# The last attention's head norms and rotations put between the units of its query projection

## The chip, the cores and the metric

The program runs on one NeuronCore of a Trainium2 chip. The metric is the device time of one execution in microseconds (us). All inputs and outputs are float32, and the whole network below is one launch.

## The reference

Two blocks of two layers each are computed on 512 tokens of width 1024; the second block also carries 256 context tokens. The change touches the last attention only, the mixer of the second block's last layer. Cut to that:

```python
def c_mixer(h_ctx, h_lat, w_in, q_norm_g, k_norm_g, w_out, need_ctx):
    def project(h):
        q, k, v = jnp.split(h @ w_in, [C_WIDTH, C_WIDTH + C_KV_WIDTH], axis=-1)
        q = rms_norm_2(q.reshape(b, t, C_HEADS, C_HEAD_DIM), q_norm_g)      # 8 heads of 128
        k = rms_norm_2(k.reshape(b, t, C_KV_HEADS, C_HEAD_DIM), k_norm_g)   # 2 heads of 128
        return q, k, v.reshape(b, t, C_KV_HEADS, C_HEAD_DIM)
    q_c, k_c, v_c = project(h_ctx)
    q_l, k_l, v_l = project(h_lat)
    q_l, k_l = apply_rope(q_l, cos, sin), apply_rope(k_l, cos, sin)
    k_all = jnp.concatenate([k_c, k_l], axis=1)     # 768 keys
    ... softmax(q k^T / sqrt(128)) v, then @ w_out
```

So each of ten tiles (two of keys over 768 tokens, eight of queries over 512) is divided by the root of its mean square over the 128 features, multiplied by a gain, and, for the 512 latent tokens, turned: `x*cos + rot(x)*sin`.

## The kernel before, in words

The kernel is written engine by engine: each engine (`block.sync`, `block.tensor`, `block.scalar`, `block.gpsimd`, `block.vector`) runs its own list of instructions in the order of the text, and semaphores with explicit counts tie them. Nothing reorders it. Activations lie with the features on the 128 partitions. TensorE is PE, ScalarE is ACT, VectorE is DVE, GpSimd is POOL.

**Split products.** A projection is computed in units of 128 output features. ACT copies a unit's weights (1024 by 128) to a rounded form, `w_hi` (L1250, the helper `f`); DVE subtracts to get the rest, `w_lo` (L1923); PE multiplies hi by hi, hi by lo and lo by hi (L775 to L777), 24 matmuls for 512 tokens. The copies of weights have two places each, taken in turn, so `w_hi` of a unit waits until PE has finished the unit two before it (`act.wait_ge(a_ready...)` in `w_hi`). The result lands in one of two slots of `psA`, from which ACT copies it to SBUF and frees the slot.

**The stage of the change.** After the third MLP (`mlp2`) the hidden state is normed, and PE makes the two key units (`c_k`), the values (`c_v`, 48 float32 matmuls, L726, copied out by DVE at L2503) and the eight query units (`c_q`). Then all engines meet: `meet` drains each engine and waits on `stage_over` until all four have come. Then `head_norms("c_n", 6, 10, ...)` runs on PE, ACT and DVE over the ten tiles, queries first, in pairs: ACT squares a tile (L1250), PE multiplies by a matrix of 1/128 (`mean128`, L726) into `psA`, ACT takes Ln and then Exp of minus a half (the inverse root), DVE multiplies tile, gain and root (L2378), PE multiplies by the rotation matrix (`rot128`, L726) into `psA`, and DVE does three operations (L2388: product with the sine, which reads PSUM; L2389: tile times cosine; L2391: the sum). The mean and rotation products are float32, and the trace has two records for each such matmul. Then there is a second `meet`, and the attention `cat` starts with its first logits. POOL only takes part in the meets here (`BEFORE_MLP3` counts those before it is needed again).

In `block.tensor` the stage reads:

```python
split_linear("c_q", sH[TOK], sL[TOK], LAT)
meet(pe)
head_norms("c_n", 6, 10, lambda m: qC[:, m, :] if m < 8 else kC[:, m - 8, :], sqc, C["mean128"], C["rot128"])
meet(pe)
attention("cat")
```

The whole functions stand here:

Of the kernel before, what the change touches and what calls it, by code (L numbers as in the profile page):

```python
# [7 lines left out]
ALU = mybir.AluOpType  # L8
ACT = mybir.ActivationFunctionType
# [4 lines left out]
KD = D // P  # L14
LAT, CTX = 512, 256
TOK = LAT + CTX
LT, CT = LAT // P, CTX // P
# [13 lines left out]
C_H, C_KV = 8, 2  # L31
# [31 lines left out]
for _name, _n in ROW_SIZES:  # L63
# [18 lines left out]
          ("mlp1", GROUPS * (GH + KD)), ("ln_v3", 1),  # L82
          ("rms0", 1), ("ab", AB_UNITS), ("ab_n", 12), ("lstm", 12),
          ("ab_out", 8), ("mlp2", GROUPS * (GH + KD)),
          ("rms2", 1), ("c_k", 2), ("c_v", 2), ("c_q", 8), ("c_n", 20), ("cat", LT * C_H), ("c_out", 8),
          ("mlp3", GROUPS * (GH + KD))]
PLAN_Q = [("dsa", 4 * DSA_H), ("mla", 4 * MLA_H)]
AHEAD = {"dsa": 2, "mla": 2, "sw": 1}
# [26 lines left out]
def build(nc, d, consts, out):  # L115
    with ExitStack() as ctx:
# [18 lines left out]
        psO = ctx.enter_context(nc.psum_tensor("psO", [P, 1024], F32))  # L135

        C = {name: const[:, a:b] for name, (a, b) in CONST.items()}
        ident = C["ident"]
        eps_ln, eps_rms = C["eps"][:, 0:1], C["eps"][:, 1:2]

        def vec(name, j):
            return vecT[:, ROW[name] + j:ROW[name] + j + 1]

        cursor = [0]

        def area(*shape, at=None):

            if at is not None:
                cursor[0] = at
            n = 1  # L150
            for s in shape:
                n *= s
            v = work[:, cursor[0]:cursor[0] + n]
            cursor[0] += n
            assert cursor[0] <= WORK, cursor[0]
            if len(shape) == 2:
                return v.rearrange("p (a b) -> p a b", b=shape[1])
            if len(shape) == 3:
                return v.rearrange("p (a b c) -> p a b c", b=shape[1], c=shape[2])
            if len(shape) == 4:  # L160
                return v.rearrange("p (a b c e) -> p a b c e", b=shape[1], c=shape[2], e=shape[3])
            return v

        def split(name, shape, at):
# [19 lines left out]
        sH, sL = ({n: split(f"{h}{n}", [P, KD, n], (1 + e) * KD * n) for n in (LAT, TOK)}  # L184
                  for e, h in enumerate(("act_hi", "act_lo")))
# [65 lines left out]

        mixT3 = area(KD, LAT, at=0)
        qC, vC, kC = area(KD, LAT, at=3 * KD * TOK), area(6, 256, at=4 * KD * TOK), area(C_KV, TOK, at=0)
        sqc, rsc, rtc = area(4, TOK), area(2, TOK), area(2, LAT)
        prob3, turn3 = area(2, TOK), area(2, TOK)
        on3 = area(LT, D, at=3 * KD * LAT)


# [10 lines left out]
        stage_over = sem("stage_over")  # L269
        out_set, out_stored = sem("out_set"), sem("out_stored")  # L270
        S = {n: sem(n) for n in (
            "centered", "squared", "sum_ready", "sum_read", "mean_read", "acc_set", "acc_mean", "ple_set", "tile_sum", "norm_set", "acc_zero", "relu_used", "gate_used", "act_hi", "act_split", "w_hi", "w_split", "g_hi", "hidden_set",
            "ada_used", "ada_sum", "row_ready", "row_set", "row_turned", "conv_set", "vec_set", "sqrt_set", "lam_exp", "lam_set",
            "dsa_max", "mla_max", "sw_max", "cat_max", "rope_raw", "root_set", "head_sq",
            "onat_set", "kr_set", "rot_set", "rot_used", "log_set", "row_arg", "carry_arg", "decay_masked", "decay_set", "gain_set", "query_set",
# [53 lines left out]
        def meet(eng):  # L329

            met[eng.engine] = met.get(eng.engine, 0) + 1
            eng.drain().then_inc(stage_over, 1)
            eng.wait_ge(stage_over, 4 * met[eng.engine])
# [25 lines left out]
        w = d["hy_w_in"][0]  # L359
# [20 lines left out]
        w = d["mla_w_down"][0]  # L380
# [3 lines left out]
        w = d["mla_w_uq"][0]  # L384
# [9 lines left out]
        w = d["mla_w_ukv"][0]  # L394
# [6 lines left out]
        w = d["ab_w_in_2"][0]  # L401
# [15 lines left out]
        w = d["c_w_in_2"][0]  # L417
# [118 lines left out]
        def swa_v(qt, kb, h):  # L536
# [19 lines left out]
                        v=lambda qt, kb, h: vC[:, kb, (h // 4) * P:(h // 4) * P + P], prob=prob3,  # L556
                        turn=turn3, onat=lambda qt: on3[:, qt, :], sink=False),
        }
        n_o = {"dsa": 0, "mla": 4, "sw": 12, "cat": 18}
        nmax, rsum, rinv, sink, sarg = small[:, 0:64], small[:, 64:128], small[:, 128:192], small[:, 192:200], small[:, 200:248]  # L560
        sp4, lz, ls, ls2, lacc = (small[:, 232 + 4 * i:236 + 4 * i] for i in range(5))
# [151 lines left out]
        def _(pe):  # L713
# [95 lines left out]
            def split_linear(stage, x_hi, x_lo, n, wait=None, units=KD, behind=None, first=0):  # L809
                if wait:  # L810
                    split_pair(stage, n, x_hi, x_lo, wait)
                for u in range(2 if wait else first, units):
                    pe.wait_ge(S["w_split"], BASE_W[stage] + u + 1)
                    hi, lo = split_place(wH, stage, u), split_place(wL, stage, u)
                    split_products(stage, [u], n, lambda j, k: (hi[:, k, :], lo[:, k, :], x_hi[:, k, :], x_lo[:, k, :]))
                    if behind and u >= 2:
                        behind(u - 2)
                if behind:
                    behind(units - 2)
                    behind(units - 1)  # L820
# [145 lines left out]
            def head_norms(stage, first, n, tile, sq, mean, rot):  # L966

                def norm(m):
                    w = tile(m).shape[-1]
                    pe.wait_ge(S["head_sq"], first + m + 1)  # L970
                    product(stage, norm_product(n, m), [(a, b, [(mean, sq[:, m % 4, a:b])])
                                                        for a, b in ((0, 512), (512, w)) if b > a])

                norm(0)
                norm(1)
                for p in range(0, n, 2):
                    for m in range(p + 2, min(p + 4, n)):
                        norm(m)
                    for m in (p, p + 1):
                        pe.wait_ge(S["rope_raw"], first + m + 1)  # L980
                        product(stage, rope_product(n, m), [(0, LAT, [(rot, tile(m)[:, 0:LAT])])])
# [232 lines left out]
            for step in lstm_steps:  # L1214
                u = step[0]
# [14 lines left out]
            w = weights(pe, "cin", 0)  # L1230
            for g in range(2):
                product("c_v", g, [tokens(w, 256, 512, hraw, t, 256 * (t - 4 * g)) for t in range(4 * g, min(4 * g + 4, 6))])
            split_linear("c_q", sH[TOK], sL[TOK], LAT)
            meet(pe)
            head_norms("c_n", 6, 10, lambda m: qC[:, m, :] if m < 8 else kC[:, m - 8, :], sqc, C["mean128"], C["rot128"])
            meet(pe)
            attention("cat")
            split_linear("c_out", sH[LAT], sL[LAT], LAT, split_here("c_out"), behind=mean_square_of(3, "c_out"))
# [9 lines left out]
        def _(act):  # L1248
# [399 lines left out]
            def head_norms(stage, first, n, tile, sq, rs):  # L1648

                def square(m):  # L1650
                    x = tile(m)
                    f(sq[:, m % 4, 0:x.shape[-1]], x, ACT.Square).then_inc(S["head_sq"], 1)

                square(0)
                square(1)
                for p in range(0, n, 2):
                    for m in range(p + 2, min(p + 4, n)):
                        square(m)
                    if p >= 2:
                        act.wait_ge(S["rope_raw"], first + p)  # L1660
                    roots = [rs[:, m % 2, 0:tile(m).shape[-1]] for m in (p, p + 1)]
                    for m in (p, p + 1):
                        ps, free = get_a(act, stage, norm_product(n, m))
                        f(roots[m % 2], ps[:, 0:roots[m % 2].shape[-1]], ACT.Ln, bias=eps_rms).then_inc(free, 1)
                    act.drain()
                    for m in (p, p + 1):
                        f(roots[m % 2], roots[m % 2], ACT.Exp, scale=-0.5).then_inc(S["root_set"], 1)
# [47 lines left out]

            rms(2, 1, 0, TOK, hraw, sH[TOK], ahead=[("c_k", 0), ("c_k", 1)])
            c_units = [("c_k", m) for m in range(2)] + [("c_q", m) for m in range(8)]
            for n in range(len(c_units) + 2):
                if 2 <= n < len(c_units):
                    w_hi(*c_units[n])  # L1720
                if n >= 2:
                    name, m = c_units[n - 2]
                    ps, free = get_a(act, name, m)
                    dst = kC[:, m, :] if name == "c_k" else qC[:, m, :]
                    f(dst, ps[:, 0:dst.shape[-1]], ACT.Copy).then_inc(free, 1)
            meet(act)
            head_norms("c_n", 6, 10, lambda m: qC[:, m, :] if m < 8 else kC[:, m - 8, :], sqc, rsc)
            meet(act)
            attention("cat", lambda t: mixT3[:, t, :], out="c_out")
            split_linear("c_out", square_of("c_out", LAT), start=2)  # L1730
# [79 lines left out]
        def _(v):  # L1810
# [686 lines left out]


            rms(2, 1, "norm1", 0, TOK, hraw, "cin", ahead=[("c_k", 0), ("c_k", 1)])
            for g in range(2):  # L2500
                n = 4 if g == 0 else 2
                ps, free = get_a(v, "c_v", g)
                nc.vector.tensor_copy(vC[:, 4 * g:4 * g + n, :],  # L2503
                                      ps[:, 0:256 * n].rearrange("p (t c) -> p t c", c=256)).then_inc(free, 1)
            for u in range(8):
                w_lo("c_q", u)
            meet(v)
            head_norms("c_n", 6, 10, lambda m: qC[:, m, :] if m < 8 else kC[:, m - 8, :], rsc, rtc,
                       lambda m: cq8 if m < 8 else vec("ck", 0), C["cosC"], C["sinC"])
            meet(v)  # L2510
            attention("cat")
            gated("c_out", 1, LAT, mixT3)
# [10 lines left out]


LRU_HALF = 8.0 / 2
BEFORE_MLP3 = 2


def host_constants():
# [88 lines left out]
```

## Time and profile before

| | us |
|---|---|
| median of 3 runs | 3305.35 |
| lowest and highest | 3304.45, 3305.71 |
| the profiled execution's own time | 3304.75 |
| its span, first to last instruction | 3303.0 |

| engine | busy, us | share of the span |
|---|---|---|
| PE, matmuls | 3107.6 | 94% |
| PE, weight loads (beside the matmuls) | 2483.6 | 75% |
| DVE | 1632.8 | 49% |
| ACT | 1238.2 | 37% |
| POOL | 155.1 | 5% |

The mean granted TensorE clock is 0.969 of full speed, and the 16 DMA engines move 259.17 MB. The times in the rows below are microseconds from the span's start. A share such as PE's 94% is a mean over very different stages; what a stage is worth is read from its own stretch. The profiled execution's time is 1.75 us above its span, and 0.60 us below the median.

### The profile page before, as it was taken

To read this page: it belongs to the slowest core of one execution; us is meant where nothing else is said; L and a number is where in the kernel's file an instruction comes from. 1 tells how busy PE (TensorE), PEld (TensorE's weight loads), DVE (VectorE), ACT (ScalarE), POOL (GpSimd) and SP (SyncE) were. 2 spreads that over 40 slices of the span, in tenths; PEclk is the share of its full clock that TensorE was granted. 3 is DMA by queue.
4 is the path that set the end of the run, shared out by engine and by line. 5 is a ranking of instruction groups with operands and counts; after the bars stand their busy time and mean duration, and the time that the engine had idled before them with its cause. 6 is when DMAs were issued, how large, how long until landed. Compare 5 with 4: busy or idle time off the path is not lost. (4 is left out here: it accounts for less than half of the span.)

```text
span 3303.0 us, 39562 instructions
## 1 busy us (share of the span) xinstructions
PE 3107.6 (94%) x15192; PEld 2483.6 (75%) x15192; DVE 1632.8 (49%) x2422; ACT 1238.2 (37%) x2046; POOL 155.1 (5%) x142
## 2 busy tenths in 40 slices
PE   6989999999998999998998998999999898899999
PEld 5666677776776677776885777788888775778887
DVE  4763666665454566674415543433333615344344
ACT  2543233335563233336114442423222424543332
POOL 2200000011000000000002001000000100000000
PEclk9969999999999999999998999999999999999999
DMA  5101443433201434431201001112121120022221
GB/s 189 52 25 40 178 157 136 177 106 52 77 1 58 175 124 178 152 109 39 64 26 52 1 1 52 51 51 76 51 76 51 51 77 0 1 77 102 102 87 65
DMA packets 157679, 259.17 MB, mean 78 GB/s; under 512 B 54332, under 2 KB 70074, under 8 KB 157436
## 3 DMA queue, kind: packets, MB, share of 16 engines
q1 hardware_dynamic: 155812, 252.66, 21.8%
q10 hardware_dynamic: 1628, 4.76, 0.4%
q8 instruction: 71, 1.16, 0.1%
q14 instruction: 40, 0.33, 0.0%
q0 software_dynamic: 128, 0.26, 0.0%
HBM read 255.57 MB, written 2.10 MB: 78 GB/s over the span
## 5 line engine op out<-in xcount | busy, mean ns | idle before, releaser
L1250 ACT ACTIVATE w_hi<-wbuf 128x1024 fp32r<-128x1024 f32 (+1 forms) x349 | 368.1, 1057 | 1227.4 <-PE psA L777 1163.9
L775 PE MATMUL psA<-act_hi,w_hi 128*128 128x512 f32 (+1 forms) x1872 | 707.5, 378 | 62.4 <-DVE act_lo L1929 37.1
L1923 DVE TENSOR_TENSOR w_lo<-wbuf,w_hi 128x1024 fp32r<-128x1024 f32 (+1 forms) x349 | 429.3, 1233 | 556.2 <-ACT w_hi L1250 551.0
L776 PE MATMUL psA<-act_lo,w_hi 128*128 128x512 f32 (+1 forms) x1872 | 701.4, 375 | 0.0
L777 PE MATMUL psA<-act_hi,w_lo 128*128 128x512 f32 (+1 forms) x1872 | 700.5, 374 | 0.0
L775 PE MATMUL psA<-hid_hi,w_hi 128*128 128x512 f32 (+1 forms) x1280 | 476.8, 373 | 5.4 <-DVE work L2032 4.5
L776 PE MATMUL psA<-hid_lo,w_hi 128*128 128x512 f32 (+1 forms) x1280 | 472.1, 369 | 0.0
L777 PE MATMUL psA<-hid_hi,w_lo 128*128 128x512 f32 (+1 forms) x1280 | 471.4, 368 | 0.0
L775 PEld LDWEIGHTS psA<-act_hi,w_hi 128*128 128x128 f32 x1872 | 358.8, 192 | 134.7 <-issue 52.1
L777 PEld LDWEIGHTS psA<-act_hi,w_lo 128*128 128x128 f32 x1872 | 357.7, 191 | 62.7
L776 PEld LDWEIGHTS psA<-act_lo,w_hi 128*128 128x128 f32 x1872 | 359.0, 192 | 60.9 <-issue 0.2
L2032 DVE TENSOR_TENSOR work<-work,psA 128x512 f32<-128x512 f32 (+1 forms) x256 | 192.8, 754 | 289.8 <-PE psA L777 282.0
L775 PEld LDWEIGHTS psA<-hid_hi,w_hi 128*128 128x128 f32 x1280 | 241.2, 188 | 65.6 <-issue 18.1
L777 PEld LDWEIGHTS psA<-hid_hi,w_lo 128*128 128x128 f32 x1280 | 241.1, 188 | 41.1
L776 PEld LDWEIGHTS psA<-hid_lo,w_hi 128*128 128x128 f32 x1280 | 241.4, 189 | 38.7
L2054 DVE SCALAR_TENSOR_TENSOR work<-work,small 128x768 f32<-128x768 f32 x224 | 221.7, 1031 | 1.5
L1250 ACT ACTIVATE work<-psA 128x512 f32<-128x512 f32 (+2 forms) x239 | 150.5, 633 | 163.0 <-PE psA L777 146.2
L1250 ACT ACTIVATE work<-psA,small 128x128 f32<-128x128 f32 (+6 forms) x232 | 128.6, 573 | 209.6 <-DVE small L1902 80.3
L2028 DVE TENSOR_TENSOR hid_lo<-work,hid_hi 128x512 fp32r<-128x512 f32 (+1 forms) x128 | 97.1, 759 | 187.0 <-ACT hid_hi L1250 187.0
L740 PE MATMUL psB<-const,work 128*128 128x128 f32 x814 | 143.6, 302 | 41.5 <-ACT work L1250 15.5
L740 PEld LDWEIGHTS psB<-const,work 128*128 128x128 f32 x814 | 102.9, 152 | 95.8 <-issue 36.9
L1250 ACT ACTIVATE work<-work 128x512 f32<-128x512 f32 (+4 forms) x236 | 150.7, 650 | 27.0 <-DVEq L2433 7.4
(271 smaller groups left out, 3562.8 us busy)
## 6 DMA issues: line engine op xcount, KB each, us to landing
wbuf<-in_mlp_w_dram SPq DMA_DIRECT2D x64, 2048.0 KB, 8.2
work<-in_ada_w_dram SPq DMA_DIRECT2D x32, 1536.0 KB, 10.9
wbuf<-in_ab_w_in_dram SPq DMA_DIRECT2D x10, 1024.0 KB, 5.0
wbuf<-in_ple_w_gate_dram SPq DMA_DIRECT2D x4, 2048.0 KB, 7.6
wbuf<-in_hy_w_in_dram SPq DMA_DIRECT2D x3, 2048.0 KB, 13.6
wbuf<-in_c_w_in_dram SPq DMA_DIRECT2D x3, 2048.0 KB, 7.6
wbuf<-in_hy_w_out_dram SPq DMA_DIRECT2D x2, 2048.0 KB, 7.8
wbuf<-in_mla_w_out_dram SPq DMA_DIRECT2D x2, 2048.0 KB, 8.3
```

What stands on the lines that cost most here:

```text
L740: ins = pe.transpose(psB[0:m, s, col:col + k], src, ident[0:k, 0:k])
L775: pe.matmul(psA[:, s, a:b], w_hi, x_hi[:, a:b], start=first, stop=False)
L776: pe.matmul(psA[:, s, a:b], w_hi, x_lo[:, a:b], start=False, stop=False)
L777: ins = pe.matmul(psA[:, s, a:b], w_lo, x_hi[:, a:b], start=False, stop=last)
L1250: return nc.scalar.activation(out, in_, func, **kw)
L1923: tt(split_target(wL, stage, u), unit(v, stage, u, g), split_target(wH, stage, u), ALU.subtract).then_inc(S["w_split"], 1)
L2028: tt(gL[n][:, m, :], hid[n][:, m % 2, :], gH[n][:, m, :], ALU.subtract).then_inc(S["hidden_set"], 1)
L2032: tt(acc[:, j, :], acc[:, j, :], ps[:, 0:n], ALU.add).then_inc(free, 1)
L2054: ins = stt(adas[:, x, :], adaw[:, e, r, :], c, adas[:, x, :], ALU.mult, ALU.add)
```

## The change

It takes the second meeting out and spreads `head_norms` over the query units. The ten tiles have a new order (`C_TILES`): tiles 0 and 1 are the keys, tiles 2 to 9 are query units 0 to 7.

- PE: a mean product is `c_norm(i)`, into `psO[:, 0:512]` (a key's reaches to column 768), and a rotation is `c_rotate(i)`, into `psO[:, 512:1024]`. There is one place for each, no longer two slots of `psA`. `c_norm(i)` waits for the square of tile i and for the root of tile i-1; `c_rotate(i)` waits for tile i to be normalized and, by `c_rot_used`, for DVE to have read the rotation of tile i-1. Ahead of unit 0 stands `c_norm(0)`; behind unit u stand `c_rotate(u-1)` and `c_norm(u+1)`; behind unit 7 the rest follows.
- ACT: behind the copy of a tile comes its square, and then the root (`c_root`) of the tile before it.
- DVE: `w_lo` of query units 0 and 1 moves ahead of the copies of the values. Each later `w_lo(u)` is followed by `c_normalize(u-2)` and, from u = 4 on, `c_turn(u-4)`, the three rotation operations.
- `rtc` and `prob3`/`turn3` move to other places in SBUF, because `act_hi` and `act_lo` are now still in use. `BEFORE_MLP3` is 1. The 20 places of `c_n` in the table of `psA` slots go; the number is even, so later slots stay as they were.

The number of operations of each kind and their shapes are the same in both kernels. The diff, cut:

```diff
-        sqc, rsc, rtc = area(4, TOK), area(2, TOK), area(2, LAT)
-        prob3, turn3 = area(2, TOK), area(2, TOK)
+        sqc, rsc = area(4, TOK), area(2, TOK)
+        rtc = area(2, LAT, at=3 * KD * TOK + KD * LAT)
+        prob3, turn3 = area(2, TOK, at=KD * TOK), area(2, TOK)
...
+        C_TILES = [(8 + m, kC[:, m, :]) for m in range(C_KV)] + [(m, qC[:, m, :]) for m in range(C_H)]
...
-            split_linear("c_q", sH[TOK], sL[TOK], LAT)
-            meet(pe)
-            head_norms("c_n", 6, 10, lambda m: qC[:, m, :] if m < 8 else kC[:, m - 8, :], sqc, C["mean128"], C["rot128"])
+            def c_norm(i):
+                w = C_TILES[i][1].shape[-1]
+                pe.wait_ge(S["head_sq"], 6 + i + 1)
+                if i >= 1:
+                    pe.wait_ge(S["root_set"], 6 + i)
+                for a, b in ((0, 512), (512, w)):
+                    if b > a:
+                        ins = pe.matmul(psO[:, a:b], C["mean128"], sqc[:, i % 4, a:b], start=True, stop=True)
+                ins.then_inc(S["c_mean"], 1)
+            def c_rotate(i):
+                pe.wait_ge(S["rope_raw"], 6 + i + 1)
+                if i < C_KV:
+                    pe.wait_ge(S["root_set"], 6 + C_KV)
+                if i >= 1:
+                    pe.wait_ge(S["c_rot_used"], i)
+                pe.matmul(psO[:, 512:512 + LAT], C["rot128"], C_TILES[i][1][:, 0:LAT], start=True, stop=True).then_inc(S["c_rot"], 1)
+            c_norm(0)
+            for u in range(C_H):
+                split_linear("c_q", sH[TOK], sL[TOK], LAT, None, u + 1, first=u)
+                if u >= 1:
+                    c_rotate(u - 1)
+                c_norm(u + 1)
+            c_rotate(7)
+            c_norm(9)
+            c_rotate(8)
+            c_rotate(9)
...
+            def c_root(i):
+                act.wait_ge(S["c_mean"], i + 1)
+                if i >= 2:
+                    act.wait_ge(S["rope_raw"], 6 + i - 1)
+                root = rsc[:, i % 2, 0:C_TILES[i][1].shape[-1]]
+                f(root, psO[:, 0:root.shape[-1]], ACT.Ln, bias=eps_rms)
+                act.drain()
+                f(root, root, ACT.Exp, scale=-0.5).then_inc(S["root_set"], 1)
...
                     f(dst, ps[:, 0:dst.shape[-1]], ACT.Copy).then_inc(free, 1)
-            meet(act)
-            head_norms("c_n", 6, 10, lambda m: qC[:, m, :] if m < 8 else kC[:, m - 8, :], sqc, rsc)
+                    act.drain()
+                    f(sqc[:, (n - 2) % 4, 0:dst.shape[-1]], dst, ACT.Square).then_inc(S["head_sq"], 1)
+                if n >= 3:
+                    c_root(n - 3)
+            c_root(9)
...
+            w_lo("c_q", 0)
+            w_lo("c_q", 1)
...
-            for u in range(8):
+            def c_normalize(i):
+                m, x = C_TILES[i]
+                v.wait_ge(S["root_set"], 6 + i + 1)
+                stt(x, x, cq8 if m < 8 else vec("ck", 0), rsc[:, i % 2, 0:x.shape[-1]], ALU.mult, ALU.mult).then_inc(S["rope_raw"], 1)
+            def c_turn(i):
+                x = C_TILES[i][1][:, 0:LAT]
+                v.wait_ge(S["c_rot"], i + 1)
+                tt(rtc[:, i % 2, :], psO[:, 512:512 + LAT], C["sinC"], ALU.mult).then_inc(S["c_rot_used"], 1)
+                tt(x, x, C["cosC"], ALU.mult)
+                v.drain()
+                tt(x, x, rtc[:, i % 2, :], ALU.add)
+            for u in range(2, 8):
                 w_lo("c_q", u)
-            meet(v)
-            head_norms("c_n", 6, 10, lambda m: qC[:, m, :] if m < 8 else kC[:, m - 8, :], rsc, rtc,
-                       lambda m: cq8 if m < 8 else vec("ck", 0), C["cosC"], C["sinC"])
+                c_normalize(u - 2)
+                if u >= 4:
+                    c_turn(u - 4)
+            for i in range(6, 10):
+                c_normalize(i)
+                c_turn(i - 2)
+            c_turn(8)
+            c_turn(9)
...
-BEFORE_MLP3 = 2
+BEFORE_MLP3 = 1
```

Where the instructions stand. First DVE before, around the value copies (L2503) and the weight rests of the query units (L1923); L2378 is the normalizing, L2388 the first operation of a turn:

```order
L1929 TENSOR_TENSOR act_lo_52<-work,act_hi_50 128x768 [waits act_hi] x2
L2503 COPY work<-psA 128x1024 [waits a_ready1]
L2503 COPY work<-psA 128x512 [waits a_ready0]
L1923 TENSOR_TENSOR w_lo<-wbuf,w_hi 128x1024 [waits w_landed1,w_hi] x4
L1923 TENSOR_TENSOR w_lo<-wbuf,w_hi 128x1024 [waits w_landed0,w_hi] x4
L2378 SCALAR_TENSOR_TENSOR work<-work,small 128x512 [waits root_set,stage_over]
L2378 SCALAR_TENSOR_TENSOR work<-work,small 128x512 [waits root_set] x3
L2388 TENSOR_TENSOR work<-psA,const 128x512 [waits a_ready1]
```

The same place on DVE in the changed kernel, where L1968 is `w_lo`, L2557 the normalizing and L2563 the first operation of a turn; the last five rows are the round of query unit 4:

```order
L1968 TENSOR_TENSOR w_lo<-wbuf,w_hi 128x1024 [waits w_landed1,w_hi] x2
L2550 COPY work<-psA 128x1024 [waits a_ready1]
L2550 COPY work<-psA 128x512 [waits a_ready0]
L1968 TENSOR_TENSOR w_lo<-wbuf,w_hi 128x1024 [waits w_landed1,w_hi]
L2557 SCALAR_TENSOR_TENSOR work<-work,vecT 128x768 [waits root_set]
L1968 TENSOR_TENSOR w_lo<-wbuf,w_hi 128x1024 [waits w_landed1,w_hi]
L2557 SCALAR_TENSOR_TENSOR work<-work,vecT 128x768 [waits root_set]
L1968 TENSOR_TENSOR w_lo<-wbuf,w_hi 128x1024 [waits w_landed0,w_hi]
L2557 SCALAR_TENSOR_TENSOR work<-work,small 128x512 [waits root_set]
L2563 TENSOR_TENSOR work<-psO,const 128x512 [waits c_rot]
L2564 TENSOR_TENSOR work<-work,const 128x512
L2566 TENSOR_TENSOR work<-work 128x512
```

The eight weight rests stood in one row, and now each is followed by a normalizing and, from unit 4 on, by a turn; the turn of a round stands behind the weight rest of that round.

On PE in the changed kernel, the end of query unit 2 and the start of unit 3 (L778 to L780 are the split products, L1255 the rotation, L1245 the mean):

```order
L778 MATMUL psA<-act_hi_50,w_hi 128x512
L779 MATMUL psA<-act_lo_52,w_hi 128x512
L780 MATMUL psA<-act_hi_50,w_lo 128x512
L1255 MATMUL psO<-work,const 128x512 [waits c_rot_used,root_set,rope_raw]
L1245 MATMUL psO<-work,const 128x512 [waits root_set,head_sq]
L778 MATMUL psA<-act_hi_50,w_hi 128x512 [waits a_free0,w_split]
L779 MATMUL psA<-act_lo_52,w_hi 128x512
```

Before, the rows L775, L776 and L777 of one unit were followed at once by those of the next. Now a rotation with its wait for `c_rot_used` and a mean product stand between them.

## Rows read from the trace of the kernel before

**Rows 1.** The page: the span.

```profile
span 3303.0 us, 39562 instructions
```

**Rows 2.** Busy time and granted clock by stretch, around this stage.

```profile
core 0: us, PE busy (x) PEld busy (x) DVE busy (x) ACT busy (x) POOL busy (x), PEclk, DMA share, GB/s
2629.60:2635.80 6.20, 6.10 (x19) 5.26 (x20) 6.02 (x10) 5.70 (x9) 0.00 (x0) 0.50 0.00 0
...
2672.10:2679.40 7.30, 7.28 (x25) 5.85 (x26) 1.10 (x1) 0.00 (x0) 0.00 (x0) 0.77 0.74 281
2679.40:2717.60 38.20, 38.17 (x169) 31.28 (x167) 7.35 (x6) 9.87 (x13) 0.00 (x0) 1.00 0.31 110
2717.60:2756.80 39.20, 22.07 (x44) 7.20 (x44) 26.52 (x40) 19.54 (x31) 0.00 (x0) 0.94 0.00 0
2756.80:2762.10 5.30, 5.21 (x8) 2.58 (x9) 0.96 (x1) 0.99 (x2) 0.00 (x0) 0.50 0.00 0
```

**Rows 3.** Timeline of PE: start, us, instruction [idle before <-releaser]; projection units.

```profile
2629.70 0.76 PE L775 MATMUL psA<-act_hi,w_hi 128*128 128x512 f32 x1 [6.24 <-DVE act_lo L1929]
...
2669.83 0.38 PE L726 MATMUL psA<-wbuf,work 128*128 128x256 f32 x1
2672.12 0.50 PE L775 MATMUL psA<-act_hi,w_hi 128*128 128x512 f32 x1 [1.91 <-DVE w_lo L1923]
...
2673.87 0.63 PE L775 MATMUL psA<-act_hi,w_hi 128*128 128x512 f32 x1
...
2679.33 0.39 PE L775 MATMUL psA<-act_hi,w_hi 128*128 128x512 f32 x1
...
2717.19 0.39 PE L777 MATMUL psA<-act_hi,w_lo 128*128 128x512 f32 x1
```

**Rows 4.** Timeline of ACT: weight copies and unit copies of the query units.

```profile
2679.59 1.06 ACT L1250 ACTIVATE w_hi<-wbuf 128x1024 fp32r<-128x1024 f32 x1 [28.26 <-PE psA L777]
2680.56 0.58 ACT L1250 ACTIVATE work<-psA 128x512 f32<-128x512 f32 x1
2685.03 1.06 ACT L1250 ACTIVATE w_hi<-wbuf 128x1024 fp32r<-128x1024 f32 x1 [3.89 <-PE psA L777]
```

**Rows 5.** Timeline of DVE: weight rests of the query units.

```profile
2680.69 1.23 DVE L1923 TENSOR_TENSOR w_lo<-wbuf,w_hi 128x1024 fp32r<-128x1024 f32 x1 [7.48 <-ACT w_hi L1250]
```

**Rows 6.** Timeline of PE between the meetings: mean and rotation products, first logits.

```profile
2719.05 1.96 PE L726 MATMUL psA<-work,const 128*128 128x512 f32 x4 [1.48 <-ACT work L1250]
...
2728.16 1.10 PE L726 MATMUL psA<-work,const 128*128 128x512 f32 x2 [1.38 <-DVE work L2388]
...
2741.55 1.53 PE L726 MATMUL psA<-work,const 128*128 128x512 f32 x4 [1.67 <-DVE work L2388]
...
2751.60 1.80 PE L726 MATMUL psA<-work,const 128*128 128x512 f32 x2 [0.87 <-DVE work L2388]
2756.89 1.22 PE L726 MATMUL psA<-work 128*128 128x512 f32 x1 [3.48 <-DVEq L332]
```

**Rows 7.** Timeline of DVE between the meetings.

```profile
2722.54 1.42 DVE L2378 SCALAR_TENSOR_TENSOR work<-work,small 128x512 f32<-128x512 f32 x2 [13.43 <-ACT work L1250]
...
2727.33 0.68 DVE L2388 TENSOR_TENSOR work<-psA,const 128x512 f32<-128x512 f32 x1
2727.94 0.68 DVE L2389 TENSOR_TENSOR work<-work,const 128x512 f32<-128x512 f32 x1
...
2756.07 0.69 DVE L2391 TENSOR_TENSOR work<-work 128x512 f32<-128x512 f32 x1
```

**Rows 8.** Timeline of ACT between the meetings: a logarithm, then exponentials and squares.

```profile
2731.26 0.69 ACT L1250 ACTIVATE work<-psA,const 128x512 f32<-128x512 f32 x1 [1.22 <-PE psA L726]
2732.03 2.62 ACT L1250 ACTIVATE work<-work 128x512 f32<-128x512 f32 x4
```

**Rows 9.** Waits between 2717.6 and 2756.9: who for whom, us, times, longest.

```profile
PE psA L726 <- DVE work L2388: 10.2, 8, 2.4
PE psA L726 <- ACT work L1250: 3.6, 4, 1.6
```

More of the change, by code:

```diff
@@ L84 @@
           ("ab_out", 8), ("mlp2", GROUPS * (GH + KD)),
-          ("rms2", 1), ("c_k", 2), ("c_v", 2), ("c_q", 8), ("c_n", 20), ("cat", LT * C_H), ("c_out", 8),
+          ("rms2", 1), ("c_k", 2), ("c_v", 2), ("c_q", 8), ("cat", LT * C_H), ("c_out", 8),
           ("mlp3", GROUPS * (GH + KD))]
@@ L253, in build @@
         qC, vC, kC = area(KD, LAT, at=3 * KD * TOK), area(6, 256, at=4 * KD * TOK), area(C_KV, TOK, at=0)
-        sqc, rsc, rtc = area(4, TOK), area(2, TOK), area(2, LAT)
-        prob3, turn3 = area(2, TOK), area(2, TOK)
+        sqc, rsc = area(4, TOK), area(2, TOK)
+        assert cursor[0] <= KD * TOK
+        rtc = area(2, LAT, at=3 * KD * TOK + KD * LAT)
+        prob3, turn3 = area(2, TOK, at=KD * TOK), area(2, TOK)
         on3 = area(LT, D, at=3 * KD * LAT)
@@ L271, in build @@
         S = {n: sem(n) for n in (
-            "centered", "squared", "sum_ready", "sum_read", "mean_read", "acc_set", "acc_mean", "ple_set", "tile_sum", "norm_set", "acc_zero", "relu_used", "gate_used", "act_hi", "act_split", "w_hi", "w_split", "g_hi", "hidden_set",
+            "centered", "squared", "sum_ready", "sum_read", "mean_read", "acc_set", "acc_mean", "ple_set", "tile_sum", "c_mean", "c_rot", "c_rot_used", "norm_set", "acc_zero", "relu_used", "gate_used", "act_hi", "act_split", "w_hi", "w_split", "g_hi", "hidden_set",
             "ada_used", "ada_sum", "row_ready", "row_set", "row_turned", "conv_set", "vec_set", "sqrt_set", "lam_exp", "lam_set",
@@ L1723, in _ @@
                     ps, free = get_a(act, name, m)
-                    dst = kC[:, m, :] if name == "c_k" else qC[:, m, :]
+                    dst = C_TILES[n - 2][1]
                     f(dst, ps[:, 0:dst.shape[-1]], ACT.Copy).then_inc(free, 1)
-            meet(act)
-            head_norms("c_n", 6, 10, lambda m: qC[:, m, :] if m < 8 else kC[:, m - 8, :], sqc, rsc)
+                    act.drain()
[3 more added lines that the diff above has]
+            c_root(9)
             meet(act)
```

## The prediction

> **What bounds the kernel now.** PE runs almost without a pause, so I first looked for the places where it does pause. The busy time by stretch [rows 2] shows the query units of this stage as solid PE work: 38.17 of 38.20 us. Behind them lie 39.20 us in which PE is busy 22.07 us, and that figure counts the overlapping ends of matmuls. The timeline of PE [rows 6] says what that stretch is: mean and rotation products with gaps between them, from the first at 2719.05 to the first logits at 2756.89. The list of waits [rows 9] puts 10.2 us of its gaps on DVE (L2388, the operation that frees a rotation's slot) and 3.6 us on ACT. The bound there is the chain PE, ACT, DVE, not any engine. It is the idle time that this change is after, so the question is what the new order makes PE wait for. I counted the stage from the end of the value product (its last record starts at 2669.83 and the next could start at 2670.05) to the first logits: 2756.89 - 2670.05 = 86.8 us [rows 3, 6].
>
> **Prices.** Between two units, 24 split matmuls apart, ACT's weight copies stand 5.44 us apart (2679.59, 2685.03) [rows 4], so a query unit is 5.44 us of PE at full clock. One mean or rotation product over 512 tokens is the difference of four records and two, 1.96 - 1.10 = 0.86 us [rows 6]. A key's mean product has 768 columns; the row with four records that take 1.53 us is one, less the 0.24 us by which the last overlaps what follows: 1.29 us. On DVE a weight rest starts 1.10 us after the weight copy (2679.59 to 2680.69) and takes 1.23 us [rows 4, 5]. A normalizing takes 0.67 us of the queue (1.42 for two, and 0.75 for a single one), and the first operation of a turn 0.68 us [rows 7]. PE starts 0.15 us after that operation has ended (2728.01 to 2728.16) [rows 6, 7]. On ACT a logarithm takes 0.69 us, and the exponential behind it starts 0.08 us later and takes about 0.60 [rows 8].
>
> **The change, part by part.** The number of operations stays, so the sum is a new timetable of this stage.
>
> 1. *The start.* The weight rests of query units 0 and 1 move ahead of the value copies on DVE. Before, PE sat 1.91 us until the first of them was ready, and unit 0 then ran partly at half rate and took 2679.33 - 2672.12 = 7.21 us [rows 3]. Now `c_norm(0)` follows the values at once. The 1.9 us and the 1.8 us both go. POOL and SP have nothing in this stage, and no DMA is issued later than it is needed, as weights for these units have landed.
>
> 2. *PE's own work in line.* Eight units are 43.5 us. Between them stand two key means (2 x 1.29) and, behind units 1 to 6, a rotation and a mean each (6 x 1.72 = 10.3): 56.4 us to the end of unit 7. ACT has some 3.6 us of work per unit and DVE some 4.0, so neither is the bound by its sum.
>
> 3. *The new wait.* The order of instructions shows that behind unit u PE meets `c_rotate(u-1)`, which waits until DVE has read the rotation of tile u-2. DVE does that in the round of `w_lo(u+2)`, behind that weight rest and behind a normalizing. And `w_lo(u+2)` needs `w_hi(u+2)`, which ACT can only write when PE has finished unit u, since the two places of the weights are taken in turn [rows 4]. So for u = 2, 3, 4, 5 PE must sit from the end of unit u through: 0.26 to the weight copy (2679.33 to 2679.59), 1.10, a rest 1.14 (its 1.23 less the overlap with the next), a normalizing 0.67, the turn's first operation 0.68, 0.15 to PE. That is 4.00 us, four times: 16.0 us. Queued behind it on PE are a mean product and the whole next unit. Behind unit 1 there is no such wait (rotation 0 has no predecessor). Behind units 6 and 7 the turns belong to rounds without a weight rest: they wait for a root that is ready 3.3 us after the unit before, well inside the unit's 5.44 us. Unit 7 thus ends at 56.4 + 16.0 = 72.4 us instead of 47.4 (2717.42).
>
> 4. *The tail.* After unit 7: rotation 6 and mean 8 (to 1.72), then ACT's root 8 (result 0.2 later, 0.69 + 0.08 + 0.60: to 3.3), normalizing 8 and the first operation of turn 6 (to 4.8). Only then rotation 7 and mean 9 (4.9 to 6.6), root 9 (to 8.25), normalizing 9 and turn 7's first operation (to 9.65), rotation 8 (to 10.7), turn 8's first operation (10.95 to 11.6), rotation 9 (11.8 to 12.85), three operations and the drain (to 15.1). The logits start 15.15 us behind unit 7 instead of 39.4. The meeting itself cost 0.13 us before (DVE ends at 2756.76), so a meeting less is worth that only.
>
>    Without the clock: 72.4 + 15.2 = 87.6 against 86.8, **0.8 us slower**. The 24 us won in the tail are paid for by work moved in line (12.9), four waits (16.0), less the repaired start (3.9).
>
> 5. *The clock.* No row shows four waits of 4 us in turn. After 1.91 us of idle PE, the granted clock of the next stretch was 0.77 on average: a spell at 1.2 GHz, in which a matmul record takes 0.63 us and not 0.39, and the unit lost 1.8 us [rows 2, 3]. After 6.24 us of idle, 6.2 us were granted 0.50 throughout [rows 2, 3], a loss of 3.1 us. Between these, and nearer the first, I take 2.4 us for each wait: 9.6 us (bounds 7.2 and 12.4, and nothing for a wait that happens to draw no spell: the stretch between the meetings, with gaps of 0.9 to 1.7 us [rows 6], was still granted 0.94 on average [rows 2]). In the tail PE waits three times some 3 us, and four products of 0.86 us stand on the chain; at half rate each costs 0.86 more, 0 to 3.4; I take 1.7. The logits start at half rate before [rows 2] and will do so now.
>
>    The Trainium skill (TensorE: Matmul & The Clock Gate, "HAM oscillation — how this bites in real kernels") says that a loop whose rounds each hold a long wait pays for the return to full clock in every round, and measured 1.67 us at half rate each. By its figure the four waits would cost 4 x 0.83 = 3.3 us and the sum would be 6 us, an estimate. The unit that lost 1.8 us after less than 2 us of idle [rows 3] speaks for the larger price, and the sum goes by the rows.
>
>    **Sum: 0.8 + 9.6 + 1.7 = 12.1 us** on the profiled execution's 3304.75 (span 3303.0 [rows 1]), that is 3316.9, and I give 3317.0. The median of the runs is 0.6 us above that execution, within the runs' own spread of 1.3 us.
>
> **The rivals.**
>
> - *The same waits, a kind clock.* If some waits fall so that no spell at 1.2 GHz follows, the clock costs 0 to 5 us and the kernel ends at 3305.5 to 3310.5; I put it at 3309. For it: the 0.94 just named. Against: these waits are more than twice as long.
> - *The waits are not there, and it is faster.* The mechanism is that of the name: what is three tiles behind is ready in time. The place is `c_rotate(u-1)`. Its price is the 16.0 us and the clock with them: 56.4 + 15.2 = 71.6 against 86.8, 15.2 us faster, 3289.6. It decides at the point where DVE reads the old rotation before unit u ends. For it: DVE has 4.0 us of work in a round of 7.2. Against: DVE works in order, and the turn stands behind a weight rest that cannot start before that unit ends. That is read from the order and from ACT's waits of 3.89 us for PE [rows 4].
> - *It feeds on itself.* If slow products also lengthen the tail and the rounds of units 6 and 7 (a root that is not ready in time), two more waits of 2 to 4 us come, with their spells: 3323 to 3330.
>
> That the change might not do what it says is ruled out by the rows of the order: the products do stand between the units.
>
> **How the numbers follow.** My forecast has 0.68, the kind clock 0.14, the faster case 0.07, the self-feeding one 0.11. The measurement of this kernel can tell about 0.2%, or 6.6 us, from no change: the bounds are 3298.7 and 3312.0. Faster is the second rival, 0.07. Within lie nearly all of the kind clock and a little of the forecast's low end, 0.14. Slower is the rest, 0.79. The range runs from 3307, which takes in most of the kind clock, to 3322, which is the forecast with each clock price at its upper bound (0.8 + 12.4 + 3.4 = 16.6, so 3321.4); outside are the faster case, a part of the self-feeding one and the best of the kind clock. The likeliest case alone spans 3312 to 3321.
>
> **What would show it.** In the new timeline of PE: no idle time between the values and unit 0, and no spell at 1.2 GHz in it; behind units 2 to 5, four times, some 4.0 us of idle released by the turn's first operation (L2563), and a granted clock below 1 behind each; nothing behind units 1, 6 and 7 before rotation 7; the first logits 15 to 18 us behind unit 7. The list of waits should show PE waiting for L2563 some 22 to 25 us in this stage. I am wrong if the gaps are under 2 us, if there are six and not four, or if the clock stays at 1.00.

## The result, and the profile after

The changed kernel takes 3320.02 us (median of 5 runs, 3317.84 to 3322.15); the kernel before takes 3305.71 us in the same comparison (3304.45 to 3310.17). The ratio is 1.0042, with a 95% interval of 1.0027 to 1.0056. The change costs 14.3 us; the forecast was 12.1.

The profiled execution has a span of 3318.2 us against 3303.0 [rows 1], 15.2 us more. The stage, counted from the end of the value product to the first logits, is read from the timeline of PE. These are its mean products (L1245), rotations (L1255) and first logits (L729); the split matmuls of the units lie between the rows:

```profile
2671.55 1.45 PE L1245 MATMUL psO<-work,const 128*128 128x512 f32 x4
2678.32 1.46 PE L1245 MATMUL psO<-work,const 128*128 128x512 f32 x4
2685.07 1.02 PE L1255 MATMUL psO<-work,const 128*128 128x512 f32 x2
2685.93 1.02 PE L1245 MATMUL psO<-work,const 128*128 128x512 f32 x2
...
2696.22 2.05 PE L1255 MATMUL psO<-work,const 128*128 128x512 f32 x2 [3.82 <-DVE work L2563]
2698.05 1.92 PE L1245 MATMUL psO<-work,const 128*128 128x512 f32 x2
...
2710.33 2.04 PE L1255 MATMUL psO<-work,const 128*128 128x512 f32 x2 [3.82 <-DVE work L2563]
...
2724.24 2.05 PE L1255 MATMUL psO<-work,const 128*128 128x512 f32 x2 [3.82 <-DVE work L2563]
...
2738.06 2.05 PE L1255 MATMUL psO<-work,const 128*128 128x512 f32 x2 [3.82 <-DVE work L2563]
...
2747.77 1.02 PE L1255 MATMUL psO<-work,const 128*128 128x512 f32 x2
...
2754.95 1.02 PE L1255 MATMUL psO<-work,const 128*128 128x512 f32 x2
2755.81 1.02 PE L1245 MATMUL psO<-work,const 128*128 128x512 f32 x2
2759.78 1.66 PE L1255 MATMUL psO<-work,const 128*128 128x512 f32 x2 [2.95 <-DVE work L2563]
...
2772.35 5.26 PE L729 MATMUL psA<-work 128*128 128x512 f32 x8 [2.18 <-DVEq L334]
```

The stage lasts 2772.35 - 2671.55 = 100.8 us, where it lasted 86.8 [rows 3, 6]: 14.0 of the 15.2 us are here, and the value product already ended 1.5 us later than before, in work that the change does not touch. Four rotations start behind 3.82 us of idle PE, each released by DVE's L2563. Before the first four rows there is no idle time. Unit 7 ends at 2754.95, which is 83.4 us into the stage (47.4 before), and the logits start 17.4 us behind it (39.5 before).

What DVE does in one such wait, from its timeline (unit 2 ended at 2692.23; ACT's weight copy started at 2692.49):

```profile
2693.58 1.23 DVE L1968 TENSOR_TENSOR w_lo<-wbuf,w_hi 128x1024 fp32r<-128x1024 f32 x1 [5.01 <-ACT w_hi L1281]
2694.72 0.75 DVE L2557 SCALAR_TENSOR_TENSOR work<-work,small 128x512 f32<-128x512 f32 x1
2695.38 0.68 DVE L2563 TENSOR_TENSOR work<-psO,const 128x512 f32<-128x512 f32 x1
```

DVE sat idle for 5.01 us, although the rotation that it would read had long been made; the first thing in its queue was the weight rest. The read that frees PE stands third. From the end of the unit to PE's start at 2696.22 it is 3.99 us.

The clock, by stretches of the changed kernel (columns as in [rows 2]): the start up to the first wait, the four rounds behind the waits, unit 7, the tail, the first logits:

```profile
2671.50:2692.20 20.70, 20.70 (x85) 15.63 (x84) 5.00 (x5) 8.95 (x12) 0.00 (x0) 1.00 0.43 156
...
2696.20:2706.40 10.20, 10.18 (x28) 6.66 (x28) 1.16 (x2) 1.32 (x2) 0.00 (x0) 0.71 0.00 0
...
2710.30:2720.20 9.90, 9.87 (x28) 6.52 (x28) 1.17 (x2) 1.32 (x2) 0.00 (x0) 0.72 0.00 0
...
2724.20:2734.10 9.90, 9.86 (x28) 6.41 (x28) 1.19 (x2) 1.32 (x2) 0.00 (x0) 0.73 0.01 2
...
2738.00:2747.80 9.80, 9.74 (x29) 6.59 (x30) 3.85 (x6) 1.32 (x2) 0.00 (x0) 0.74 0.58 212
2747.80:2754.90 7.10, 7.10 (x29) 5.24 (x28) 2.65 (x4) 2.54 (x4) 0.00 (x0) 1.00 0.00 0
2754.90:2772.30 17.40, 8.49 (x13) 2.34 (x12) 9.22 (x14) 3.86 (x6) 0.00 (x0) 0.75 0.00 0
2772.30:2777.60 5.30, 5.25 (x9) 2.64 (x10) 0.96 (x1) 0.99 (x2) 0.00 (x0) 0.53 0.00 0
```

The rounds behind the waits are granted 0.71 to 0.74, and PE is busy in them without a break. A rotation and a mean behind a wait take 2.05 and 1.92 us, not 1.02 each. A rotation, a mean and a unit take 7.17 us at full rate (2685.07 to 2692.24), and the four rounds last 10.1, 9.9, 9.8 and 9.7 us, so the spells at 1.2 GHz cost 10.9 us in all, 2.5 to 3.0 us each. The list of waits of PE in the stage:

```profile
PE psO L1255 <- DVE work L2563: 22.1, 7, 3.8
PE psA L729 <- DVEq L334: 2.2, 1, 2.2
```

Before, PE waited 10.2 us for L2388 and 3.6 for ACT between the meetings [rows 9]. The change took those waits out and put 22.1 us on the same kind of operation.

### The profile page after: what moved, and what is told of

Its sections match the earlier page's. It is cut to its first block, busy times and chain, and to the rows that moved or that the text cites. A ratio compares the mean times of both kernels' runs of the same rounds, so it can differ in the third digit from the quotient of the medians.

```text
span 3318.2 us, 39574 instructions
## 1 busy us (share of the span) xinstructions
PE 3119.2 (94%) x15192; PEld 2490.5 (75%) x15192; DVE 1633.9 (49%) x2422; ACT 1239.2 (37%) x2046; POOL 154.2 (5%) x142
## 4 chain that ended last, share of the span: by engine, by line
PE 86%; DVE 6%; ACT 4%; issue 1%; DVEq 1%; DMA 1%; ACTq 1%; POOLq 0%; PEldq 0%; PEld 0%; SPq 0%
PE psA L778 23%; PE psA L779 22%; PE psA L780 22%; PE psB L743 3%; PE psA L729 3%; PE psA L904 2%; PE psO L921 2%; ACT work L1281 2%; PE psO L1045 1%; PE psO L866 1%; PE psA L965 1%; ACT w_hi L1281 1%; DVE w_lo L1968 1%; PE psA L794 1%; DVE work L2077 1%
## 5 line engine op out<-in xcount | busy, mean ns | idle before, releaser
L778 PE MATMUL psA<-act_hi,w_hi 128*128 128x512 f32 (+1 forms) x1872 | 712.8, 381 | 60.3 <-DVE act_lo L1974 37.0
L1968 DVE TENSOR_TENSOR w_lo<-wbuf,w_hi 128x1024 fp32r<-128x1024 f32 (+1 forms) x349 | 430.4, 1236 | 580.5 <-ACT w_hi L1281 575.1
L780 PE MATMUL psA<-act_hi,w_lo 128*128 128x512 f32 (+1 forms) x1872 | 700.9, 374 | 0.0
L778 PE MATMUL psA<-hid_hi,w_hi 128*128 128x512 f32 (+1 forms) x1280 | 476.8, 373 | 5.4 <-DVE work L2077 4.5
L780 PE MATMUL psA<-hid_hi,w_lo 128*128 128x512 f32 (+1 forms) x1280 | 471.5, 368 | 0.0
L778 PEld LDWEIGHTS psA<-act_hi,w_hi 128*128 128x128 f32 x1872 | 359.5, 192 | 134.8 <-issue 54.4
L780 PEld LDWEIGHTS psA<-act_hi,w_lo 128*128 128x128 f32 x1872 | 358.5, 192 | 63.2
L778 PEld LDWEIGHTS psA<-hid_hi,w_hi 128*128 128x128 f32 x1280 | 241.2, 188 | 65.7 <-issue 18.2
L780 PEld LDWEIGHTS psA<-hid_hi,w_lo 128*128 128x128 f32 x1280 | 241.1, 188 | 41.3
## 6 DMA issues: line engine op xcount, KB each, us to landing
work<-in_ada_w_dram SPq DMA_DIRECT2D x32, 1536.0 KB, 10.9
```

What stands on the lines that cost most here:

```text
L778: pe.matmul(psA[:, s, a:b], w_hi, x_hi[:, a:b], start=first, stop=False)
L780: ins = pe.matmul(psA[:, s, a:b], w_lo, x_hi[:, a:b], start=False, stop=last)
L1968: tt(split_target(wL, stage, u), unit(v, stage, u, g), split_target(wH, stage, u), ALU.subtract).then_inc(S["w_split"], 1)
```

## The experiments

Eight kernels ran, in two groups of four, each beside the kernel before, whose median was 3305.84 us in the first group and 3306.03 in the second. The stage is measured as above in each one's profile.

| kernel | median, us | against before, 95% | stage, us | unit 7's end, us | logits behind it, us |
|---|---|---|---|---|---|
| before | 3305.71 | 1 | 86.8 | 47.4 | 39.5 |
| the change | 3320.02 | 1.0042 (1.0027 to 1.0056) | 100.8 | 83.4 | 17.4 |
| turn before the weight rest | 3293.56 | 0.9961 (0.9945 to 0.9976) | 74.9 | 56.6 | 18.4 |
| turn first everywhere | 3286.97 | 0.9946 (0.9930 to 0.9961) | 67.3 | 56.6 | 10.8 |
| two places for a rotation | 3290.05 | 0.9952 (0.9937 to 0.9968) | 69.3 | 56.6 | 12.7 |
| filled waits | 3310.17 | 1.0013 (1.0004 to 1.0022) | 88.8 | 72.8 | 16.0 |
| the start alone | 3302.23 | 0.9991 (0.9982 to 1.0000) | 84.2 | 43.8 | 40.4 |
| two tiles behind | 3283.76 | 0.9930 (0.9917 to 0.9944) | 66.9 | 57.4 | 9.4 |
| two behind, filled end | 3287.19 | 0.9937 (0.9924 to 0.9951) | 66.8 | 57.4 | 9.4 |
| half-filled waits | 3312.28 | 1.0018 (1.0009 to 1.0028) | 94.0 | 76.1 | 17.9 |

(In the row of the start alone, the stage is counted from the first query matmul at 2675.82, since PE goes from the values straight to it.)

### The turn before the weight rest

```diff
             for u in range(2, 8):
+                if u >= 4:
+                    c_turn(u - 4)
                 w_lo("c_q", u)
                 c_normalize(u - 2)
-                if u >= 4:
-                    c_turn(u - 4)
```

> The changed kernel, but in each round DVE makes the turn first and the weight rest behind it, so the old rotation is read before the unit ends. My theory (PE waits four times for a turn that is queued behind a weight rest that needs the unit's end): the four gaps of 3.8 us go, and with them the spells at 1.2 GHz behind them (10.9 us); the stage from the value product's end to the first logits falls from 100.8 us to 56.4 + 17.4 = 73.8, and the time from 3320 to 3291 to 3294, under the kernel before. The rival (PE is slowed by float32 products standing between the units, whatever DVE does) expects the gaps to shrink little and at most 5 us off: 3315 or more.

It took 3293.56 us, in the expected range. The same three DVE operations, in another place of the same round, and all four gaps are gone. Two stretches of its profile, the units and the tail:

```profile
2672.50:2729.10 56.60, 56.60 (x226) 42.15 (x225) 25.41 (x33) 25.02 (x36) 0.00 (x0) 1.00 0.32 112
2729.10:2747.40 18.30, 9.38 (x13) 2.53 (x11) 9.25 (x14) 3.86 (x6) 0.00 (x0) 0.72 0.00 0
```

PE is busy in all of the 56.60 us, at full clock. The forecast's timetable had 56.4 for this work without waits. So float32 products between the units cost their own 0.86 and 1.29 us and 0.2 us beyond that in all, and the rival that blamed them falls. Against the change, the stage is 25.9 us shorter: 16.0 of waits and 10.9 of spells, less 1.0 by which this tail is longer.

### The turn first everywhere

```diff
             for i in range(6, 10):
-                c_normalize(i)
                 c_turn(i - 2)
+                c_normalize(i)
```

This stands on top of the edit before.

> As the first, and the turn stands ahead of the normalizing in the last rounds too, so that rotation 7 and mean 9 do not wait for root 8 and normalizing 8. My theory: rotation 7 starts about 2 us behind unit 7 and no longer 4.8, and the logits start 11 to 13 us behind unit 7 and not 17.4: 3286 to 3289. If the tail is bound by the sum of DVE's own operations, not by their order, it stays within 1 us of the first.

It took 3286.97 us. The tail fell from 18.4 to 10.8 us, just under the expected 11 to 13. The last products in its timeline of PE:

```profile
2728.43 1.02 PE L1255 MATMUL psO<-work,const 128*128 128x512 f32 x2
2729.29 1.02 PE L1245 MATMUL psO<-work,const 128*128 128x512 f32 x2
2730.33 1.10 PE L1255 MATMUL psO<-work,const 128*128 128x512 f32 x2
2731.88 1.10 PE L1245 MATMUL psO<-work,const 128*128 128x512 f32 x2 [0.45 <-ACT work L1281]
2733.27 1.10 PE L1255 MATMUL psO<-work,const 128*128 128x512 f32 x2 [0.29 <-DVE work L2563]
2735.93 1.10 PE L1255 MATMUL psO<-work,const 128*128 128x512 f32 x2 [1.56 <-DVE work L2563]
2739.21 4.54 PE L729 MATMUL psA<-work 128*128 128x512 f32 x8 [2.18 <-DVEq L334]
```

Rotation 7 starts 1.9 us behind unit 7's end, where it started 4.8 in the change. The long way through mean 8, root 8, normalizing 8 and the turn, twice over, was a matter of order as well. Part of the 7.6 us is the clock: the last four products take 1.10 us each here, and 1.78 to 2.05 us each in the run before.

### Two places for a rotation

```diff
-                if i >= 1:
-                    pe.wait_ge(S["c_rot_used"], i)
-                pe.matmul(psO[:, 512:512 + LAT], C["rot128"], C_TILES[i][1][:, 0:LAT], start=True, stop=True).then_inc(S["c_rot"], 1)
+                if i >= 2:
+                    pe.wait_ge(S["c_rot_used"], i - 1)
+                pe.matmul(psB[:, i % 2, :], C["rot128"], C_TILES[i][1][:, 0:LAT], start=True, stop=True).then_inc(S["c_rot"], 1)
...
-                tt(rtc[:, i % 2, :], psO[:, 512:512 + LAT], C["sinC"], ALU.mult).then_inc(S["c_rot_used"], 1)
+                tt(rtc[:, i % 2, :], psB[:, i % 2, :], C["sinC"], ALU.mult).then_inc(S["c_rot_used"], 1)
```

DVE's order is that of the change.

> The changed kernel with DVE's order left as it is, but with two places for a rotation (in psB, by the tile's parity), so that a rotation waits for the turn two tiles back. It tells the single place apart from the order on DVE. My theory: the gaps go just as in the first, 56.4 us to the end of unit 7, and the tail is about 13 us: 3286 to 3291. If the order on DVE is itself the bound, the gaps stay: 3315 or more.

It took 3290.05 us, and unit 7 ends 56.6 us into the stage. The rotations behind units 2 and 3, in its timeline of PE, have no idle time before them:

```profile
2690.24 1.02 PE L1255 MATMUL psB<-work,const 128*128 128x512 f32 x2
...
2697.42 1.02 PE L1255 MATMUL psB<-work,const 128*128 128x512 f32 x2
```

The wait needs both: one place, and a reader that is queued behind something that needs the end of the unit. Either remedy takes it out whole.

### The waits filled

```diff
+                if 2 <= u <= 5:
+                    keep_clock(psB[:, 0, :], 4)
                 if u >= 1:
                     c_rotate(u - 1)
                 c_norm(u + 1)
```

> The changed kernel with four idle-filling float32 matmuls (their result is not used) ahead of the rotation behind units 2 to 5: 3.44 us of PE work in each wait of 3.8. The waits stay, the clock should not fall. My theory: the rotations start within 0.3 us of where they do now, counted from their unit's end, but the rounds last 11.2 us and not 13.8 to 14.1, and the time falls by the clock's 10.9 us to 3308 to 3311. If the clock costs only the 3.3 us by the Trainium skill's figure, 3316 to 3318; if the rounds are long for another reason, no change.

It took 3310.17 us, 9.9 under the change. Two of the four waits in its timeline of PE, with the filling matmuls at L734:

```profile
2697.08 3.60 PE L734 MATMUL psB<-const 128*128 128x512 f32 x8
2701.06 1.10 PE L1255 MATMUL psO<-work,const 128*128 128x512 f32 x2 [0.39 <-DVE work L2565]
2702.00 1.02 PE L1245 MATMUL psO<-work,const 128*128 128x512 f32 x2
2708.31 3.60 PE L734 MATMUL psB<-const 128*128 128x512 f32 x8
2712.30 1.10 PE L1255 MATMUL psO<-work,const 128*128 128x512 f32 x2 [0.38 <-DVE work L2565]
```

The rotation still starts 3.98 us behind the unit's end (2697.08 to 2701.06), so the wait is all there. But the round from one rotation to the next is 11.24 us and not 14.11, and the granted clock from 2697 to 2755 is 1.00. Unit 7 ends 72.8 us into the stage; the forecast had 72.4 without the clock. This measures the two parts apart: unit 7 ends 16.2 us later than where nothing waits (56.6), which is the waiting, and 10.6 us earlier than in the change (83.4), which is what the half rate behind the waits cost. The Trainium skill's figure (TensorE: Matmul & The Clock Gate, "HAM oscillation — how this bites in real kernels"), carried over to these four waits, gave 3.3 us by an estimate; these runs disagree with that and the measurement decides. That every round pays anew, as the page says, agrees: each of the four rounds of the change lost 2.5 to 3.0 us.

### The start alone

```diff
+            w_lo("c_q", 0)
+            w_lo("c_q", 1)
             for g in range(2):
...
-            for u in range(8):
+            for u in range(2, 8):
                 w_lo("c_q", u)
```

This is the kernel before with that one edit.

> The kernel before with one part of the change alone: the weight rests of query units 0 and 1 ahead of the value copies on DVE. My theory: the 1.9 us of idle PE behind the values go, and so does the spell at 1.2 GHz in unit 0 (1.8 us); the stage falls from 86.8 to 83.0 us, the time by 3 to 4 us to 3302. The rival (the gap goes but a spell falls in unit 0 anyway, or the units' start only moves a wait to the second meeting): the stage is 85 or more and the time unchanged within 1 us.

It took 3302.23 us, 3.8 less than the kernel before (3306.03 in that group), though the interval reaches to 1.0000, so the two medians alone hardly show a gain. The trace does. Its first query matmul, first mean product and first logits, in its timeline of PE:

```profile
2675.82 0.58 PE L775 MATMUL psA<-act_hi,w_hi 128*128 128x512 f32 x1
...
2721.21 1.95 PE L726 MATMUL psA<-work,const 128*128 128x512 f32 x4 [1.48 <-ACT work L1250]
...
2759.99 4.26 PE L726 MATMUL psA<-work 128*128 128x512 f32 x8 [3.53 <-DVEq L332]
```

The gap of 1.91 us and the spell in unit 0 went: from the first query matmul to the first mean product it is 45.4 us, where it was 46.9 [rows 3, 6], and the 2.1 us from the end of the values to the first query matmul are gone as well. About 0.9 us came back later: from there to the logits it is 38.8 us and was 37.8, and the granted clock between the meetings is 0.91, where it was 0.94 [rows 2]. The stage is 84.2 us, 2.7 less than before; that lies between the 83.0 of the forecast and the 85 of the rival.

### Two tiles behind

```diff
-                if u >= 1:
-                    c_rotate(u - 1)
+                c_rotate(u)
                 c_norm(u + 1)
...
+            c_normalize(0)
             for u in range(2, 8):
                 w_lo("c_q", u)
-                c_normalize(u - 2)
-                if u >= 4:
-                    c_turn(u - 4)
-            for i in range(6, 10):
-                c_normalize(i)
-                c_turn(i - 2)
+                c_turn(u - 2)
+                c_normalize(u - 1)
+            c_turn(6)
+            c_normalize(7)
+            c_turn(7)
+            c_normalize(8)
+            c_normalize(9)
             c_turn(8)
             c_turn(9)
```

Rotations have their two places in `psB`, and the mean products of queries alternate between the halves of `psO`, so a mean product waits only for the root two tiles back.

> Two places for rotations (psB) and two for the mean products, and everything one tile closer: the rotation of tile u behind unit u, turn u-2 and normalizing u-1 in DVE's round of unit u, so that one turn less is left behind unit 7. My theory: no gap between units, 56.5 us to the end of unit 7, logits 9.5 to 10.5 us behind it, against 10.8 in the run with the turn first everywhere; the stage is 66 to 67 us and the time 3284.5 to 3287. If the closer order makes PE wait for a normalizing between the units, the stage is 68 or more.

It took 3283.76 us and is the fastest of all, 22.3 us under the kernel before and some 36 under the change. There is one more product in line, so unit 7 ends 0.9 us later, and the tail is 9.4 us. The stage is 66.9 us, as expected; the time lies 0.7 us under the expected range. Its profiled execution is the slowest of its five, 3294.24 us, and the last section says where a part of its 10.5 us above the median went. Its last gap on PE, in its timeline:

```profile
2739.14 1.88 PE L1246 MATMUL psO<-work,const 128*128 128x512 f32 x4
2742.42 1.12 PE L1254 MATMUL psB<-work,const 128*128 128x512 f32 x2 [1.41 <-DVE work L2555]
2743.70 1.12 PE L1254 MATMUL psB<-work,const 128*128 128x512 f32 x2
2747.70 4.27 PE L729 MATMUL psA<-work 128*128 128x512 f32 x8 [2.87 <-DVEq L334]
```

What is left is DVE's last two turns before the meeting.

### A filled end

```diff
             c_rotate(9)
+            keep_clock(psO[:, 0:512], 3)
             meet(pe)
```

> As the run before, and three float32 matmuls whose result is not used stand behind the last rotation, where PE waits for DVE's last turns. If the half rate at which the first logits run is drawn by that idle time, they take 2.8 us and not 4.5, and 1.5 to 2.5 us are won. If the spell has already begun when the filling starts, the filling itself runs at half rate, takes 5.2 us and delays the logits by up to 2 us: nothing won or 1 us lost.

The clock answered as hoped, the median did not. The logits in its timeline of PE:

```profile
2738.65 2.74 PE L734 MATMUL psO<-const 128*128 128x512 f32 x6
2741.68 2.85 PE L729 MATMUL psA<-work 128*128 128x512 f32 x8 [0.30 <-DVEq L334]
```

They take 2.85 us and not 4.27, so the first logits are done 1.4 us earlier, counted from the start of the stage. The median is 3287.19 us all the same, 3.4 above the run without filling, whose own runs reach from 3282.78 to 3294.24. Whether the filling is worth anything in total stays open, and the expected 1.5 to 2.5 us are not shown.

### The waits half filled

The edit is that of the filled waits with 2 in the place of 4.

> The changed kernel with two instead of four filling matmuls in each of the four waits: 1.72 us of work, 2.1 us of idle left. The gap of 1.9 us behind the values before drew a spell at 1.2 GHz. If idle time as such draws it, spells follow each wait and the rounds stay near 13 us: 3315 to 3319. If it is the share of work that counts, split idle time draws fewer: rounds of 11.2 us, and 3308 to 3311 as with full filling.

It took 3312.28 us, between the two. Its four rotations behind a wait:

```profile
2694.41 1.10 PE L1255 MATMUL psO<-work,const 128*128 128x512 f32 x2 [2.10 <-DVE work L2565]
...
2705.65 1.10 PE L1255 MATMUL psO<-work,const 128*128 128x512 f32 x2 [2.10 <-DVE work L2565]
...
2716.89 1.53 PE L1255 MATMUL psO<-work,const 128*128 128x512 f32 x2 [2.10 <-DVE work L2565]
...
2729.82 1.10 PE L1255 MATMUL psO<-work,const 128*128 128x512 f32 x2 [2.10 <-DVE work L2565]
```

Four idle times of the same 2.10 us: the first two drew no spell (rounds of 11.24 us), the last two drew one (12.93 us, and 8.9 where 7.2 is the full-rate length). So neither expectation held alone.

## Why the prediction was right

The forecast was 3317.0 us, with a range of 3307 to 3322. 3320.02 lies inside it, and its mechanism is the one that the runs show.

- *The start* (step 1) was right in the change: no idle PE behind the values, full clock in unit 0. By itself it ends unit 7 3.6 us earlier (43.8 and not 47.4), where 3.9 were forecast, and shortens the stage by 2.7.
- *PE's own work in line* (step 2): 56.4 us forecast, 56.6 measured where nothing waits.
- *The new wait* (step 3): 4.00 us four times forecast, behind units 2 to 5 and nowhere else; measured 3.99, at those four places. This was the step on which the sign hung, and it came from the order of instructions: a turn behind a weight rest that needs the end of the unit.
- *The tail* (step 4): 15.15 us forecast without the clock, 16.85 with the clock's 1.7; measured 17.4. Rotation 7 was forecast 4.9 us behind unit 7 and started 4.8 behind it. (Step 5 speaks of three waits of some 3 us in the tail. Step 4's own times give two, and one of 1.1; the trace has 2.95, 2.95 and 0.88.)
- *The clock* (step 5) was the term that was undersized. I took 2.4 us for each wait, 9.6 in all, nearer the lower row; the four rounds cost 10.9 (10.6 by the filled waits). The tail's share was 2.2, not 1.7. Together that is 1.8 of the 1.9 us by which the stage's 14.0 exceed the forecast's 12.1. Both prices were picks between two bounds and not worked out, so that they came this near was partly luck. The 14.3 us between the medians need nothing more, since the five runs of either kernel differ by 4 to 6 us.
- *The rivals.* A kind clock did not come: all four waits drew spells. With half-filled waits two of four did not, so that rival was not far-fetched. What I said for it was read too kindly: between the meetings there was also a gap of 2.4 us [rows 9], and the rotation at 2751.60, the second behind it, took 1.80 us where another took 1.10 [rows 6]. The faster case, with waits that are not there, was refuted for this kernel and is exactly what the first experiment built: 3289.6 was worked out for it, and 3293.56 measured, with a tail whose clock that rival had left out. The self-feeding case did not happen: units 6 and 7 had no waits.
- *PE's waits for the turn's first operation* were forecast as 22 to 25 us and are 22.1.

## What to carry to other kernels

When work of a chain is threaded between the units of another, ask of each single buffer which instruction frees it, and what stands ahead of that instruction in its own queue: if that needs the end of the present unit, the producer waits every round, as it did here four times, although what it needed was read from a tile made a whole unit before. Put the freeing read first in the round, or give the buffer a second place; here one moved line turned 14 us lost into 12 us won. Price such a wait at more than its length: here 16.0 us of waiting brought another 10.6 to 10.9 us, lost by matmuls at half rate.

## What was not expected of the hardware

- Equal idle times are not equally dear: of four gaps of 2.10 us in one run, two were followed by matmuls at full rate and two by a spell at 1.2 GHz (rounds of 11.24 against 12.93 us), while 3.82 us drew one four times out of four. What told the two pairs of 2.10 us apart is not shown.
- Work that is the same in all kernels ends at different times: in the profiles shown here the mean product behind the values starts anywhere between 2669.55 (two places) and 2680.85 us (two tiles behind), though nothing before it differs between these two. A good part of it goes with the granted clock. From the wait of PE that ends at 1523 to 1529 us to the one that ends at 1996 to 2007, with 7.5 us of waiting before the latter in each, seven of the ten profiles take 472.3 to 473.0 us, and three (filled waits, the start alone, two tiles behind) take 477.8 to 477.9; from 1530 to 1990 us those three are granted 0.95 and the others 0.96 or 0.97. Why their clock differs is not shown. It means that a difference of 3 us between two medians of a few runs says little here, and that the length of the stage, read from the trace, is the sharper measure.
